# Decoder step: who copies the turned probabilities of the first prompt attention out of PSUM

## The reference

```python
sc = indexer_scores(iqb, iwb, ik)
sc = jnp.where(key_pos[None, None, :] <= tpos[None, :, None], sc, NEG_BIG)
val, idx = lax.top_k(sc, k_sel)            # k_sel = 256
return sparse_attend(qb, kv[bidx, idx], tpos[None, :, None] - idx, val > 0.5 * NEG_BIG, bias_a)
...
logits = einsum('ntgre,ntkge->ntgrk', qg, k) * E ** -0.5 + bias
prob = softmax(where(valid, logits, NEG_BIG));  o = einsum('ntgrk,ntkge->ntgre', prob, v)
```

## Time and profile before

| | |
|---|---|
| median of 3 runs | 3138.88 us (3137.43 to 3148.48) |
| the profiled execution | 3134.88 us, its span 3133.1 us |
| granted TensorE clock, mean | 0.973 of full speed |
| PE busy | 2971.2 us (95%) |
| VectorE busy | 1982.5 us (63%) |
| ScalarE busy | 870.2 us (28%) |
| first attention, first layer | from 445.95 us (first L2502) to 553.05 us (last L2525) |
| VectorE in 444 to 483 us | busy 36.01 of 39 us, clock 0.71 |
| PE in 483 to 510 us | busy 25.09 of 27 us, clock 0.92 |

### The profile page before, as it was taken

The page is one execution under the profiler, slowest core; times in us unless marked ns, Lnnn a source line. Parts: engine busy times, 40 slices in busy tenths (PEclk is TensorE's granted clock), DMA queues, the critical chain, the costliest instruction groups (busy, mean ns, idle before and its releaser), DMA issues.

```text
span 3133.1 us, 59139 instructions
## 1 busy us (share of the span) xinstructions
PE 2971.2 (95%) x23104; PEld 2744.0 (88%) x23120; DVE 1982.5 (63%) x3417; ACT 870.2 (28%) x1479; POOL 645.6 (21%) x754
## 2 busy tenths in 40 slices
PE   7999988999999999999989999789899999999997
PEld 6799975768899999999978999657688999999997
DVE  5798996697554444544348989867956544445444
ACT  3422113243233333300133122123323333332001
POOL 4153400001032233200041552000000333331000
PEclk9999989999999999999999999899999999999998
DMA  7343434243122222322143444353310222223322
GB/s 265 113 156 120 147 116 187 87 132 110 34 82 76 71 74 76 142 96 88 39 152 101 146 146 137 132 198 106 113 63 28 82 83 82 82 82 121 103 77 98
DMA packets 128645, 340.09 MB, mean 109 GB/s; under 512 B 20277, under 2 KB 71622, under 8 KB 123382
## 3 DMA queue, kind: packets, MB, share of 16 engines
q1 hardware_dynamic: 79426, 177.19, 15.8%
q0 software_dynamic: 33088, 102.84, 10.7%
q10 hardware_dynamic: 15844, 56.18, 5.2%
HBM read 266.10 MB, written 74.53 MB: 109 GB/s over the span
## 4 chain that ended last, share of the span: by engine, by line
PE 71%; DVE 20%; issue 3%; ACT 2%; DMA 1%; DVEq 1%; POOL 0%; SPq 0%; ACTq 0%; POOLq 0%
PE PS L1520 25%; PE PS L1542 16%; DVE U L2413 10%; PE PS L1084 7%; PE PS L1457 3%; PE PS L929 2%; PE PS L1428 2%; PE PS L1430 2%; PE PS L1429 2%; PE PS L1098 2%; PE PS L1321 2%; PE PS L1008 1%; PE PS L1030 1%; PE PS L1049 1%; DVE U L2502 1%
## 5 line engine op out<-in xcount | busy, mean ns | idle before, releaser
L2413 DVE TENSOR_SCALAR_CACHE_REDUCE U<-U,smu 32x2080 bf16<-32x2080 f32 (+6 forms) x462 | 504.8, 1146 | 13.6 <-issue 1.8
L2301 DVE TENSOR_TENSOR RGR<-WS,RGR 128x512 fp32r<-128x512 f32 x280 | 218.2, 780 | 280.8 <-ACT RGR L1602 280.2
L1520 PE MATMUL PS<-XBR,RGR 128*128 128x264 f32 x2560 | 369.2, 285 | 0.6 <-DVE RGR L2301 0.6
L1520 PE MATMUL PS<-XAR,RGR 128*128 128x264 f32 x2880 | 357.4, 285 | 1.0 <-DVE RGR L2301 1.0
L1520 PEld LDWEIGHTS PS<-XAR,RGR 128*128 128x128 f32 x2880 | 355.0, 188 | 1.4 <-DVE RGR L2301 1.4
L615 POOL DMA_DIRECT2D WS<-wjobs x176 | 94.9, 539 | 1254.7 <-PE PS L1542 492.0
L1520 PEld LDWEIGHTS PS<-XBR,RGR 128*128 128x128 f32 x2560 | 334.6, 188 | 1.1 <-DVE RGR L2301 1.1
L1602 ACT ACTIVATE U<-PS 128x528 f32<-128x528 f32 (+12 forms) x326 | 158.9, 498 | 528.3 <-PE PS L1520 234.5
L1602 ACT ACTIVATE RGR<-WS 128x512 fp32r<-128x512 f32 (+1 forms) x286 | 182.1, 637 | 261.2 <-PE PS L1520 240.3
L660 POOL TENSOR_TENSOR WS<-WS 128x512 f32<-128x512 f32 x160 | 225.6, 1416 | 130.7 <-DVE RGR L2301 60.9
L1520 PE MATMUL PS<-HnR,RGR 128*128 128x264 f32 x1280 | 207.0, 284 | 0.0
(11 more groups left out here) (346 smaller groups left out, 5459.2 us busy)
## 6 DMA issues: line engine op xcount, KB each, us to landing
WS<-wjobs POOLq DMA_DIRECT2D x113, 512.0 KB, 3.8
WS<-wjobs ACTq DMA_DIRECT2D x50, 512.0 KB, 4.5
hmid<-U SPq DMA_DIRECT2D x44, 528.0 KB, 2.6
WS<-wjobs POOLq DMA_DIRECT2D x48, 384.0 KB, 3.3
Hn<-ckT SPq DMA_DIRECT2D x16, 896.0 KB, 10.7
Hn<-hmid SPq DMA_DIRECT2D x4, 3168.0 KB, 10.8
U<-kT_pool SPq DMA_DIRECT2D x160, 64.0 KB, 2.0
xres<-U SPq DMA_DIRECT2D x2, 4224.0 KB, 16.1
```

The source lines that it names most:

```text
L1520: m = mm(out, w[:, k * P:(k + 1) * P], x[:, k, t], start=fresh and n == 0 and k == 0, stop=n == 2 and k == 3, skip_group_check=True)
L2301: tt(out=lo, in0=plain(p, i, g), in1=hi.bitcast(F32), op=ALU.subtract).then_inc(wp_lo, 1)
L2413: ts(U[0:m, JUNK[i]:JUNK[i] + w // 2].bitcast(BF16), s, CANDF[0:m, i:i + 1], None, op, ALU.add, accum_out=into[0:m, i:i + 1])
```

## The change

In the first prompt attention (`k == 0`) the turned groups of units 0 to 7 are copied by ScalarE at the end of its step, behind the exponentials and the copy of the reciprocals, and no longer by VectorE. Units 8 to 15, and all of the second attention, stay with VectorE. VectorE's first copy (unit 8) waits until all of ScalarE's are done, so that both count up the same semaphore in order. The waits on the slots and banks are the same as before; PE's list is unchanged. BY_SCALAR is TILES, 8.

```diff
+        BY_SCALAR = TILES
+
+        def turned_free(eng, G):
+            if G >= 4:
+                eng.wait_ge(at_pv, ((G - 4) // NG) * NU + GROUPS[(G - 4) % NG][0] + 1)
+
+        def turned_width(u, g):
+            return P * (min(4 * g + 4, UNITS[u][1] + 1) - 4 * g)
+
+        def turned_at(k, G):
+            return PTB[k] + (G % 4) * 512
...
                         copy(U[:, o:o + P], PS[:, 6, P:2 * P]).then_inc(at_rb, 1)
+                    if k == 0 and 1 <= s <= BY_SCALAR:
+                        for n, hh, g in mine(s - 1):
+                            w, o = turned_width(s - 1, g), turned_at(0, n)
+                            act.wait_ge(at_tr, n + 1)
+                            turned_free(act, n)
+                            copy(U[:, o:o + w], PS[:, TURN_AT[n % 3], 0:w]).then_inc(at_pt, 1)
...
                         v.reciprocal(RC[:, x:x + 2], RS[:, x:x + 2]).then_inc(at_rc, 1)
-                        for n, hh, g in mine(u):
-                            G = k * NG + n
-                            w = P * (min(4 * g + 4, UNITS[u][1] + 1) - 4 * g)
+                        if k == 0 and u == BY_SCALAR:
+                            v.wait_ge(at_pt, GT[BY_SCALAR])
+                        for n, hh, g in mine(u) if k or u >= BY_SCALAR else ():
+                            G, w = k * NG + n, turned_width(u, g)
                             v.wait_ge(at_tr, G + 1)
-                            if G >= 4:
-                                v.wait_ge(at_pv, ((G - 4) // NG) * NU + GROUPS[(G - 4) % NG][0] + 1)
-                            o = PTB[k] + (G % 4) * 512
+                            turned_free(v, G)
+                            o = turned_at(k, G)
                             v.tensor_copy(U[:, o:o + w], PS[:, TURN_AT[G % 3], 0:w]).then_inc(at_pt, 1)
```

## The result

The changed kernel takes 3148.94 us (median of 20 runs, 3142.78 to 3162.34), the kernel before 3138.08 us (20 runs, 3132.92 to 3155.76). The medians lie 10.9 us apart. The forecast was 3148.0 us.

A forecast was written before the change was run, and what follows sets the result against it. VectorE was taken to set the pace in steps 1 to 5, then a loop through VectorE and PE. Terms of -0.4 + 4.93 = +4.5 us a layer, +9.1 in all, on the 3138.88 us median gave 3148.0 us, range 3138 to 3159.

The forecast's parts named there:

- Gain 0.4 us a layer: Mask steps 1 to 5: copies off VectorE gain 0.4 us in step 1, nothing in steps 2 to 5; ends 0 and 0.5.
- Delay of PE's last group: Steps 5 to 8: PE's fourth turned group waits for ScalarE's first copy, 1.13, 1.22, 1.31 and 1.27 us later.
- They add up, and nothing takes them back: The four delays of steps 5 to 8 sum to 4.93 us a layer, with no later slack absorbing them.
- Sum: Both layers: -0.4 + 4.93 = +4.5 us a layer, +9.1 us in all, ends 8.1 and 10.8.
- The clock's play: Around step 6, PE's clock returning earlier or later: up to 1.9 us a layer either way, -3.7 to +3.7 us.
- VectorE's load: Rival, steps 1 to 5: copies really were VectorE's load, both layers save 10.3 us, 3128.6 us; chance 0.05.
- Absorbed: Rival, steps 5 to 8: PE's extra 1.2 us falls into existing idle time, -0.8 us, about 3138; chance 0.10.
- The clock falls: Rival, steps 7 and 8: PE at clock 0.5 adds up to 10 us a layer, 3168 us; chance 0.10.

The follow-up runs named there:

- the first three experiments: Against the kernel before: units 0 to 3 copied by ScalarE, first attention 106.84 us; reciprocals before exponentials in steps 2 to 5, 106.61; both together, 100.87 and 100.88.
- The dose: The change, but with only units 0 to 5 copied by ScalarE and units 6 and 7 by VectorE: first attention 108.34 and 108.57 us.
- the first experiment: The change, but with only units 0 to 3 copied by ScalarE and 4 to 7 by VectorE: first attention 106.84 us in both layers, ratio 1.0026.
- both edits at once: Kernel before with units 0 to 3 copied by ScalarE and reciprocals of steps 2 to 5 before exponentials: first attention 100.87 and 100.88 us, ratio 0.9972.
- the repeat: Units 0 to 3 copied by ScalarE, 4 to 7 by VectorE, run once more: ratio 0.9995, first attention 106.82 and 107.12 us.

## Why the prediction was right

- *Gain 0.4 us a layer.* First logits start at 447.12 (445.95 before) and those of step 5 at 480.80 (480.17): 0.54 us gained, 0.39 of it in step 1 and 0.15 in step 2, which the forecast had at 0. The claim behind it, that in steps 2 to 4 L2525 waits for ScalarE anyway, is shown by idle times of 0.98, 1.06 and 1.14 us where the copies were, and by the two-by-two of the first three experiments.
- *Delay of PE's last group.* Forecast 1.13, 1.22, 1.31, 1.27 us. Measured against the shift of each step's own logits (the group's shift less that): 484.49 - 482.78 - 0.63 = 1.08; 493.69 - 490.77 - 1.76 = 1.16; 501.48 - 497.29 - 2.92 = 1.27; 513.95 - 508.58 - 4.14 = 1.23. Together 4.74 against 4.93; the 0.90 us from the reciprocals' copy to PE's group was 0.04 to 0.06 too long each time.
- *They add up, and nothing takes them back.* The shift of the logits grows from 0.63 through 1.76, 2.92 and 4.14 to 5.36 us, and the last result row ends 5.63 us later: 4.46 us longer with the start's 1.17 off. So 0.3 us came behind step 8, where the forecast had nothing. The dose and the kernel with only the first copies on VectorE show that these four places make nearly all of the cost.
- *Sum.* Forecast 4.5 us a layer; 4.46 and 4.00. That layer 1 comes so close is partly luck: 0.54 gained instead of 0.4 and 4.74 lost instead of 4.93 would give 4.2, and the 0.3 us behind step 8 makes up for it. In layer 2 step 5 took 8.5 us instead of 8.8, as the clock came back earlier behind the logits; before, layer 2 had been 0.1 us shorter there as well. The rest of the difference between the layers, 0.3 us, lies behind the last logits. The clock's play had been bounded by 1.9 us a layer.
- *The rivals.* "VectorE's load" fails on the first experiment: 3.5 us of copies gone, 0.2 to 0.3 us gained. The Trainium skill's advice to hand work to ScalarE when VectorE is saturated ("Perfetto Trace Analysis", section "Optimizing Scalar/DVE Operations") bears fruit once ScalarE's order is changed: 7.5 us a layer against before. "Absorbed" fails on the four delays. "The clock falls" did not happen in steps 7 and 8 of the profiled execution: from 489.3 to 557.4 us the granted clock was 1.00. It did happen in the stretch behind the attention, in layer 2 only; I had no case for it. The kernel before showed no long stretch in its one profiled execution, but its runs spread by 23 us too, as far as two long stretches would take them, and those of the changed kernel by 20. Of these, the ten fastest have a mean granted clock of 0.975 to 0.977 and the ten slowest one of 0.970 to 0.974. That the long stretch makes this spread is likely by these numbers and not shown. That the forecast lies within a microsecond of the median is in part luck for that reason: 8.5 us is what the traces show for the change, the ratio says some 9, and the medians lie 10.9 apart.

## What to carry to other kernels

Before moving work off a busy engine, look at what the next instruction there waits for: if its other condition ends at the same time, the move alone gives next to nothing, and both must be moved. On the receiving engine the place in the order counted here, not the load: a short copy for which another engine waits belongs ahead of long work that is due a step later. And where one stretch takes one of two times in any execution, compare the stretch that the edit touches, not the sum.

## What the runs showed of the hardware

The stretch between the two attentions takes 74.5 to 78 us or 88.9 to 90.8 us, and nothing between. Of the twenty such stretches in the ten profiled executions eleven were long: both in the first execution with units 0 to 3, in the one with the first copy on VectorE, in the one with both edits at once and in the one with all sixteen units; one with the change, with ScalarE's copies first and in the repeat; none before, with the reciprocals early and with units 0 to 5. In a long one PE's granted clock stands at 0.50 (1.2 GHz) for 31 to 34 us while PE is busy all the time. In a short one it is at full clock there, and the times at 0.50 elsewhere in it add up to between 3.4 us (units 0 to 5, layer 2) and 13 us (before). The same 32 small products of PE before and after the place where the clock falls or doesn't, first in the kernel before (layer 1, short), then in the changed one (layer 2, long):

```profile
585.79 2.00 PE L1321 MATMUL PS<-U 64*128 64x64 f32 x32 [0.92 <-DVE U L2687]
...
588.30 2.00 PE L1321 MATMUL PS<-U 64*128 64x64 f32 x32
```

```profile
2145.85 2.00 PE L1333 MATMUL PS<-U 64*128 64x64 f32 x32 [0.92 <-DVE U L2705]
...
2148.56 3.68 PE L1333 MATMUL PS<-U 64*128 64x64 f32 x32
```

PE had the same idle time of 0.92 us in both, so that alone doesn't decide. The Trainium skill ("TensorE: Matmul & The Clock Gate", section "A second HAM failure mode: psum-queue depth-cycling") tells of a clock that swings when PE idles briefly between groups; here it stays down with no idle time in PE's rows, 30.00 us busy of 30.00. What decides between the two in one execution was not tried. Nor is it shown that an edit has no part in it: 12 more runs found no difference for one kernel, but how often each kernel has the long stretch is known from two to four profiled stretches each.

Second, the clock can be won by an edit elsewhere: with the mask steps 4.0 us shorter, PE's `scores(6)` ran at full clock in both layers of all three kernels that had it (both edits at once, copies first, all sixteen units), and at 0.50 for the most part in both layers of the kernel before. PE's weight loads had been idle for 3.2 us before it with both edits at once and for 4.4 us before. In the first of the three kernels this gave another 2.0 to 2.2 us a layer.
